# Load order of a decoder's first modulation blocks, and where the token turns and the bias vectors stand

## What is computed

```python
ada  = silu(c) @ ada_w[layer] + ada_b[layer]      # 6 x 1024 values a layer: shift, scale, gate, twice
h    = rms(x) * norm_w * (1 + scale) + shift      # scale and shift: the first 2048 of them
proj = h @ ab_w_in                                # dt, conv channels, q, k, v, z
bias = rel_bias[rel_bucket(dist)]                 # 32 x 8 table, used by both softmax mixers
```

## Time and profile before

| | |
|---|---|
| median of 3 executions | 1093.24 us (1091.28 to 1093.86) |
| the profiled execution, first to last instruction | 1092.7 us |
| PE busy, DVE busy, ACT busy | 94%, 73%, 56% |
| mean granted PE clock | 0.976 of full speed |
| DMA | 195.6 MB, mean 179 GB/s |

### The profile page before, as it was taken

How to read it: one execution, slowest core, us unless ns; L and a number is a source line. 1 busy time by engine, 2 the same in 40 slices (tenths; PEclk the granted TensorE clock), 3 DMA queues, 4 the chain that set the end, 5 groups by cost and what they waited for, 6 DMA issues and landing times.

```text
span 1092.7 us, 26456 instructions
## 1 busy us (share of the span) xinstructions
PE 1023.7 (94%) x9559; PEld 941.5 (86%) x9559; DVE 796.2 (73%) x1671; ACT 612.6 (56%) x1370; POOL 4.9 (0%) x7
## 2 busy tenths in 40 slices
PE   4899988969999999999999999999998999999997
PEld 4799977957789999887999998889887879999885
DVE  0488435686588888878788788856777988888854
ACT  2566645455476666447666684633255466666444
POOL 0000000000000000000000000000000000000000
PEclk8899989999999999999999999899999999999999
DMA  9657573643665656783577653223104856666662
GB/s 351 234 177 229 203 308 116 239 148 97 208 235 176 188 176 189 267 311 116 159 246 233 190 176 97 60 80 95 42 2 159 302 170 179 182 183 181 185 186 84
DMA packets 55115, 195.58 MB, mean 179 GB/s; under 512 B 6099, under 2 KB 8147, under 8 KB 54908
## 3 DMA queue, kind: packets, MB, share of 16 engines
q1 hardware_dynamic: 55036, 194.49, 54.2%
HBM read 193.39 MB, written 1.07 MB: 178 GB/s over the span
## 4 chain that ended last, share of the span: by engine, by line
PE 77%; DVE 12%; DMA 3%; ACT 3%; issue 3%; SPq 1%; DVEq 0%; ACTq 0%
PE proj L535 52%; PE acc L535 24%; DVE w_lo L1588 3%; DMA ada_long<-in_ada_stream 2%; DMA raw<-in_w_stream 1%; SPq L432 1%; DVE ada_pairs L1603 1%; DVE yn L1742 1%; DMA ada_ssd<-in_ada_stream 1%; ACT w_hi L1165 1%; DVE x L1749 1%; DVE ada_sum L1603 1%; PE acc L769 1%; DVE dec L2010 0%; DVE y_mix L1958 0%
## 5 line engine op out<-in xcount | busy, mean ns | idle before, releaser
L1588 DVE TENSOR_TENSOR w_lo<-raw,w_hi 128x512 fp32r<-128x512 f32 x528 | 358.6, 684 | 93.6 <-ACT w_hi L1165 92.1
L1165 ACT ACTIVATE w_hi<-raw 128x512 fp32r<-128x512 f32 x528 | 327.7, 625 | 151.3 <-PE acc L535 122.4
L535 PE MATMUL proj<-h_hi,w_hi 128*128 128x256 f32 x1408 | 403.2, 286 | 2.5 <-DVE w_lo L1588 2.0
L535 PE MATMUL proj<-h_lo,w_hi 128*128 128x256 f32 x1408 | 400.9, 285 | 4.5 <-DVE h_lo L1796 4.4
L535 PE MATMUL proj<-h_hi,w_lo 128*128 128x256 f32 x1408 | 399.9, 284 | 0.0
L535 PEld LDWEIGHTS proj<-h_lo,w_hi 128*128 128x128 f32 x1408 | 271.8, 193 | 6.7 <-DVE h_lo L1796 6.7
L535 PEld LDWEIGHTS proj<-h_hi,w_hi 128*128 128x128 f32 x1408 | 271.8, 193 | 4.9 <-issue 2.3
L535 PEld LDWEIGHTS proj<-h_hi,w_lo 128*128 128x128 f32 x1408 | 271.8, 193 | 0.0
L535 PE MATMUL acc<-w_hi,a_hi 128*128 128x512 f32 x304 | 123.5, 406 | 6.5 <-DVE y_ssd L1927 2.5
L535 PE MATMUL acc<-w_lo,a_hi 128*128 128x512 f32 x304 | 120.9, 398 | 0.0
L535 PE MATMUL acc<-w_hi,a_lo 128*128 128x512 f32 x304 | 120.3, 396 | 0.0
(11 more groups left out here) (297 smaller groups left out, 1255.4 us busy)
## 6 DMA issues: line engine op xcount, KB each, us to landing
raw<-in_w_stream SPq DMA_DIRECT2D x264, 512.0 KB, 3.6
ada_long<-in_ada_stream SPq DMA_DIRECT2D x40, 512.0 KB, 7.0
ada_first<-in_ada_stream SPq DMA_DIRECT2D x20, 512.0 KB, 4.7
ada_ssd<-in_ada_stream SPq DMA_DIRECT2D x16, 512.0 KB, 5.8
ada_out<-in_ada_stream SPq DMA_DIRECT2D x12, 512.0 KB, 4.6
ada_mid<-in_ada_stream SPq DMA_DIRECT2D x8, 512.0 KB, 7.0
hankel<-bias_scratch SPq DMA_DIRECT2D x2, 1024.0 KB, 6.0
x<-in_x_tiles SPq DMA_DIRECT2D x1, 1024.0 KB, 10.6
```

The source lines that it names most:

```text
L535: return pe.matmul(out, a, b, start=start, stop=stop, skip_group_check=True)
L1165: act.activation(hi, src, ACT.Copy).then_inc(w_rounded, 1)
L1588: dve.tensor_tensor(lo, src, hi.bitcast(F32), ALU.subtract).then_inc(w_split, 1)
```

## The change

Constants: the identity and `eps` come first in `cst`; a first transfer brings these 194 of 1473 columns, a later one the rest. SP's order becomes: `prm_rows`, first constants, blocks 0 to 3, x, blocks 4 to 11, the wait for the second quad, first halves of blocks 12 to 15 (each 256 KB), their second halves, units 0 and 1, `bucket`, `rel`, units 2 and 3, `rows`, the other constants, units 4 and 5, and only then the wait for `vec_copied`, the store, its wait, `hankel_load(0)` and unit 6 and on. `ada_quad(3)` waits for the first halves, makes 16 of its products, then waits for the second halves. One token turn stands behind the second quad and one behind the third. The bias vectors are made on PE behind unit 1 (`conv0` step 0), in the accumulator banks, and copied by ACT in step 1, that is after the end of unit 2; DVE no longer copies them, and `project_first` no longer waits.

```diff
-for _name, _n in (("ident", 128), ("ident_wrap", 64), ("ones", 128), ("triu", 128), ("triu_chunk", 128), ("same_chunk", 128), 
+for _name, _n in (("ident", 128), ("ident_wrap", 64), ("eps", 2), ("ones", 128), ("triu", 128), ("triu_chunk", 128), ("same_chunk", 128), 
...
+CST_FIRST = CST["ones"]
...
             sp.dma_start(prm_rows[:, :, :], prm_dram).then_inc(in_landed[0], 16)
-            sp.dma_start(cst[:, :], cst_dram).then_inc(in_landed[1], 16)
+            sp.dma_start(cst[:, 0:CST_FIRST], cst_dram[:, 0:CST_FIRST]).then_inc(in_landed[1], 16)
             for m in range(4):
                 load_ada(m)
             sp.dma_start(x[:, :, :], x_dram).then_inc(in_landed[2], 16)
             for m in range(4, 8):
                 load_ada(m)
-            sp.dma_start(rows[:, :], row_dram.broadcast_to([P, ROW_COLS])).then_inc(in_landed[3], 16)
+            for m in range(8, 12):
+                load_ada(m)
+            sp.wait_ge(ada_rows_mm, 2)
+            for half, landed in ((0, lambda m: ada_early), (1, lambda m: ada_landed[m % 8])):
+                cols = slice(4 * half * P, 4 * half * P + 4 * P)
+                for m in range(12, 16):
+                    sp.dma_start(ada_slots(m)[0][:, :, 4 * half:4 * half + 4].rearrange("p o a b -> p o (a b)"),
+                                 ada_dram[:, m:m + 1, cols]).then_inc(landed(m), 16)
+            load_w(0)
+            load_w(1)
             sp.dma_start(bucket[0:33, :, :], bucket_dram).then_inc(in_landed[4], 16)
             sp.dma_start(rel[0:32, :], rel_dram).then_inc(in_landed[4], 16)
-            for m in range(8, 16):
-                load_ada(m)
-            for n in range(4):
-                load_w(n)
+            load_w(2)
+            load_w(3)
+            sp.dma_start(rows[:, :], row_dram.broadcast_to([P, ROW_COLS])).then_inc(in_landed[3], 16)
+            sp.dma_start(cst[:, CST_FIRST:CST_COLS], cst_dram[:, CST_FIRST:CST_COLS]).then_inc(in_landed[5], 16)
+            load_w(4)
+            load_w(5)
             sp.wait_ge(vec_copied, 1)
             sp.dma_start(scratch, bias_vec[0:AH, :, :]).then_inc(bias_vec_stored, 16)
             sp.wait_ge(bias_vec_stored, 16)
...
-            stream(4, n_q0 + 2)
+            stream(6, n_q0 + 2)
...
             def ada_quad(i):
-                for m in range(4 * i, 4 * i + 4):
-                    pe.wait_ge(ada_landed[m % 8], 16 * (m // 8 + 1))
+                def landed():
+                    for m in range(4 * i, 4 * i + 4):
+                        pe.wait_ge(ada_landed[m % 8], 16 * (m // 8 + 1))
+
+                if i == 3:
+                    pe.wait_ge(ada_early, 64)
+                else:
+                    landed()
                 if i >= 2:
                     pe.wait_ge(ada_copied, i - 1)
                 for k in range(8):
+                    if i == 3 and k == 4:
+                        landed()
...
+            def bias_vectors():
+                pe.wait_ge(in_landed[4], 32)
+                pe.wait_ge(rel_ones, 1)
+                for v in range(2):
+                    last = mm(AB[v][0:AH, 0:384], rel[0:33, :], bucket[0:33, v, :])
+                last.then_inc(vec_mm, 1)
...
+                    if name == "conv0" and isinstance(k, int) and k == 0:
+                        bias_vectors()
                     if name[:-1] == "conv" and isinstance(k, int) and k == 1:
                         turn_dt(int(name[-1]))
...
                 ada_quad(i)
                 if i:
                     ada_turn(i - 1)
-                if i == 1:
-                    turn_x(0, 0, range(4))
-                    turn_x(0, 1, range(4))
-            pe.wait_ge(in_landed[4], 32)
-            pe.wait_ge(rel_ones, 1)
-            for v in range(2):
-                last = mm(PB[2 * v][0:AH, 0:384], rel[0:33, :], bucket[0:33, v, :])
-            last.then_inc(vec_mm, 1)
+                if i in (1, 2):
+                    turn_x(0, i - 1, range(4))
             ada_turn(3)
-            pe.wait_ge(vec_copied, 1)
             project_first(PARTS["dt0"][0], 0)
             project("conv0")
+            pe.wait_ge(in_landed[5], 16)
             bias_tiles(0)
...
                     act.activation(dst[:, ds(k, 1), :], one(ps), ACT.Identity, bias=b, scale=w).then_inc(conv_first, 1)
+                    if layer == 0 and isinstance(k, int) and k == 1:
+                        act.wait_ge(vec_mm, 1)
+                        for v in range(2):
+                            last = act.activation(bias_vec[0:AH, v], AB[v][0:AH, 0:384], ACT.Copy)
+                        last.then_inc(vec_copied, 1)
...
             def ssd():
                 gates(0)
                 dve.wait_ge(in_landed[3], 16)
+                dve.wait_ge(in_landed[5], 16)
...
             unit_x(0, 1)
-            dve.wait_ge(vec_mm, 1)
-            for v in range(2):
-                last = dve.tensor_copy(bias_vec[0:AH, v], PB[2 * v][0:AH, 0:384])
-            last.then_inc(vec_copied, 1)
             read_mods(0, 16, PB[3])
```

More of the change, by code:

```diff
@@ L75 @@
 CST, CST_COLS = {}, 0
-for _name, _n in (("ident", 128), ("ident_wrap", 64), ("ones", 128), ("triu", 128), ("triu_chunk", 128), ("same_chunk", 128),
+for _name, _n in (("ident", 128), ("ident_wrap", 64), ("eps", 2), ("ones", 128), ("triu", 128), ("triu_chunk", 128), ("same_chunk", 128),
                   ("reverse", 128), ("keep", 128), ("keep_chunk", 64), ("level", LEVELS * 64),
-                  ("ident_chunk", 64), ("pick", 255), ("eps", 1)):
+                  ("ident_chunk", 64), ("pick", 255)):
     CST[_name] = CST_COLS
     CST_COLS += _n
+CST_FIRST = CST["ones"]
 def constants():
@@ L103, in constants @@
     put("pick", np.broadcast_to(np.arange(255) == 127, (P, 255)))
-    put("eps", np.full((P, 1), EPS_COL))
+    put("eps", np.full((P, 2), EPS_COL))
     return c
@@ L255, in build @@
         tile_at = lambda k: 18 + k if k < 4 else k - 4
-        in_landed = [sem(f"in_landed{i}") for i in range(5)]
+        in_landed = [sem(f"in_landed{i}") for i in range(6)]
+        ada_early = sem("ada_early")
         bias_vec_stored, hankel_landed, out_stored = sem("bias_vec_stored"), sem("hankel_landed"), sem("out_stored")
```

## The result

The changed kernel takes 1098.2 us (median of 5 executions, 1095.1 to 1099.5), the kernel before 1091.3 beside it (5, 1090.5 to 1093.9): ratio 1.0047, 95% interval 1.0029 to 1.0065, **5.1 us slower** (3.2 to 7.1). Forecast were 1091.7 us and no difference; slower by over 0.3% had 0.06. The profiled execution took 1098.2 us, 1.8 more than its span.

A forecast was written before the change was run, and what follows sets the result against it. PE was taken to bound nearly all of the run, except the first 32 us, which hang on landing blocks and then PE. Terms -7.3 + 1.3 + 2.85 + 1.6 = -1.55 us gave 1091.7 us from the median of 1093.24, range 1088.2 to 1094.6.

The forecast's parts named there:

- I take 2.0: Start of the queue: taking 767 KB of constants out from ahead of the blocks lands block 7 2.0 us sooner.
- `rows`, `bucket` and `rel` at 2.1 us: Queue ahead of block 8: these small loads took 2.1 us, saved by putting them behind the blocks.
- Block 12 when quad 1 ends, 21.5, with block 11 still in flight: Queue in the head: SP issues block 12 at 21.5 us, before block 11 lands at about 23.3.
- I give the halves 0.3 us: Last four blocks in halves: a thinner queue costs 0.3 us, bounds 0 and 5.0; second halves land near 28.4.
- PE is the limit: Quad 3: begins near 28.7 us, after its second halves land, so PE doesn't wait; it ends at 30.7, not 36.1.
- rival (e): Blocks 12 to 15: each half takes a whole block's 1.26 us, last lands at 33.4, head 2.7, total +3.1; chance 0.03.
- Full clock for quad 3: PE in the head: split token turns keep it busy, so quad 3 takes 1.95 us at full clock, not 3.62.
- Unit 0 in time: End of the head: unit 0 lands near 29.7 us, rounded at 31 to 32; first product at 32.8, not 40.09.
- Head in sum: Everything before unit 0's first product: 7.3 us gained, range 6.0 to 8.2.
- Bias products +1.3: Between units 1 and 2 on PE: the four moved bias products and their handover cost 1.3 us.
- gap +2.85: Between units 5 and 6: SP's wait for `vec_copied` delays unit 6, PE stands 2.85 us (1.5 to 4.5).
- clock +1.6: Behind the PE gap at unit 6: half clock costs 1.6 us (0 to 2.9).

## Why the prediction was wrong

Wrong in sign; the sum was -1.55 us, the ratio says +5.1. By its own steps:

- **"I take 2.0" for 767 KB of constants: a term was missing.** Block 7 landed 0.5 us sooner in the profiles (19.23 for 19.73). The bytes were worth their price where they could be priced alone (2.4 us with the small transfer kept). What the sum put at nothing is the cost of a small transfer at the start, some 2 us of landing time: the queue ran at 209 instead of 388 GB/s behind it. No row of before shows that; why it is so stays open. `rows`, `bucket` and `rel` at 2.1 us was right: block 8 follows block 7 by 1.28 instead of 3.4.
- **"Block 12 when quad 1 ends, 21.5, with block 11 still in flight", "I give the halves 0.3 us", "PE is the limit": failed.** Quad 1 ended at 23.0 and block 11 landed 2.5 us later, but the first half that was issued then took 3.2 us to arrive, so the queue ran nearly dry. The text had the numbers for this: with blocks 1.26 us apart, block 11 would land near 22.8 (it says 23.3), 1.3 us after block 12's issue at 21.5, and a load needs the "usual 3.5". The halves landed 0.95 us apart, between the 0.63 of half a block and the 1.26 of rival (e). PE waited for them, and quad 3 ended at 34.1 instead of 30.7. The bound of 5.0 was in the text, the value was taken from its low end. Rival (e), with 0.03, had a last landing at 33.4 and a head of 2.7 us, and 32.90 and 3.3 were measured: it was the nearest of all, though by half its mechanism only.
- **Full clock for quad 3: right; that the split of the token turns is what brings it isn't shown.** It took 1.08 us for each half, against 3.62 for the whole before. But in three of the ten profiles with the head of the kernel before, both turns behind quad 1, quad 3 took 1.95 to 1.96 us as well (2.5 to 3.65 in the others); the value of the split can't be taken from one profile.
- **Unit 0 in time: half a microsecond short.** From quad 3's end to the first product it took 2.6 us, not 2.1, after ACT had stood 0.66 us for the landing of unit 0.
- **Head in sum: 3.3 instead of 7.3** (4.4 by the medians over the profiles). Both are below the range of 6.0 to 8.2 that I gave it.
- **Bias products +1.3, gap +2.85, clock +1.6: right,** at 1.4, 2.9 and 1.5, each step at its place. The removal of the gap measured 4.3 to 4.6 together. The clock's 1.6 was chosen between two stretches of before, 2.9 and 1.6, so some luck is in it.
- **The two columns of `eps`: not costed at all.** I read `("eps", 2)` as an edit of the table's order. It moved `a_hi` and `a_lo` by 32 bytes, and 912 products started about 4 to 5 ns further apart, some 4 us. No row of before shows this; but the prediction should have named the edit and said that everything allocated behind the table moves.

So -3.3 + 1.4 + 2.9 + 1.5 + 4 = 6.5 us, against a measured 5.1 (3.2 to 7.1); with the head's 4.4 over all profiles it is 5.4. With the shift undone the sum for that kernel is -4.8 + 1.4 + 3.1 + 1.5 = 1.2 us, and measured were 1.2 (ratio 1.0011). That these two agree to a tenth is luck: the same kernel's profile stands at 1.9 by the end of `conv0`, and the interval is -0.8 to 3.1. Without the shift the time, 1093.2 + 1.2 = 1094.4, would have been just inside the range of 1088.2 to 1094.6, for a head that was too good by about 3 us.

Not shown: why the gain of whole blocks ahead of unit 0 doesn't reach the medians, and which half-clock stretches later in the run belong to the change. Between 105 and 440 us the distance of the two profiles moved between 0 and +2.5, where they had half clock at different times.

## What to carry to other kernels

An edit that changes a tile's size moves every tile behind it: keep such tables at a multiple of 64 bytes (here shifts of 0 and 64 bytes were fast, 32 slow; no other was tried), or compare the time from start to start of the same products before and after, in a stretch that the edit doesn't touch. The mean duration of one product isn't enough: it was 392 to 394 ns in one profile of the fast kernel and 395 in the slow one. Ask of what leaves a queue whether what follows can fill the hole; here it didn't at the start, nor behind the wait for quad 1. And when a wait with a round trip through device memory moves into an issue order, put ahead of it as many loads as the round trip lasts: here two more units removed a gap and the half clock behind it, 4.4 us.

## What was not expected of the hardware

- Products of 128x512 whose weights (`a_hi`, `a_lo`) lie 32 bytes off their old place start 234 instead of 229 ns apart; 64 bytes off they start 227 apart. The working area was moved by 64 bytes both in a fast and in a slow kernel, so the two tiles' place matters; which of the two, and whether it is the weight load or another access, wasn't tried apart. The 256-column products show nothing of it (120 ns in all).
- At the start of the program the queue moved 209 GB/s from 4 to 6 us behind a transfer of 97 KB (776 bytes a partition), and 388 behind one of 864 KB (209 to 266 in six kernels, 371 to 395 in twelve).
- Halves of 256 KB landed 0.95 us apart, whole blocks of 512 KB 1.27.
- A store of 24 KB to device memory and the wait for it took 1.64 us from issue to the next issue, with another 6.1 us from issue to landing for a load issued behind the 1 MB read.
